# Eight-row transfers for half of three units in the expert stage

## The chip, the cores and the metric

One NeuronCore of a Trainium2 chip runs the whole kernel. The metric is the device time of one execution in microseconds, and the kernel before has a median of 1470.73 us over three runs (1468.03 to 1473.0). One further execution was taken with the hardware profiler; all rows below come from it.

## The reference

Two layers of a hybrid backbone on 256 latent and 256 context tokens of width 1024, all in float32. Each layer has a mixer (attention heads beside a convolution module) and a channel layer: a dense SwiGLU in layer 0, and in layer 1 a top-2-of-8 expert SwiGLU on the latent tokens alone, which is the stage that the change touches:

```python
def swiglu(h, w1, w3, w2):
    return (jax.nn.silu(h @ w1) * (h @ w3)) @ w2

def moe_swiglu(h, w_r, b_r, w1, w3, w2):
    hf = h.reshape(B * L, D)                                   # 256 x 1024
    logits = (hf @ w_r).astype(jnp.float32) + b_r
    top_v, top_i = lax.top_k(logits, TOP_K)                    # 2 of 8
    gates = jax.nn.softmax(top_v, axis=-1)
    combine = jnp.sum(jax.nn.one_hot(top_i, N_EXPERTS) * gates[..., None], axis=-2)
    out = jnp.zeros_like(hf)
    for e in range(N_EXPERTS):
        out = out + combine[:, e:e+1] * swiglu(hf, w1[e], w3[e], w2[e])
    ...
# w1, w3: (8, 1024, 2816), w2: (8, 2816, 1024)
```

The three weight arrays of the eight experts are 8 x 3 x 1024 x 2816 x 4 bytes, 277 MB, and each is read once. After the experts come the residual sum and a last RMSNorm with its store.

## The kernel before, in words

The work of layer 0 and of layer 1's mixer comes first; the expert stage runs from about 795 us to the end. Its weights come through a ring in the on-chip memory that holds 18 pieces, called units (`UNITS_HELD`, `RING_AT`). An expert is cut into three groups of columns (`WIDTH` 768, 1024, 1024), so that there are 24 groups g. A group has eight units of first weights (`H_UNIT[g, p, m]`: w3 and w1 for four pairs of 128-row blocks of the input, 128 partitions x 2 x 768 or 1024 numbers) and three or four units of w2 (`Y_UNIT[g, u]`: 256 rows of w2, 128 partitions x 2 x 1024 numbers, 1 MB). The order, the same for the loads and for TensorE, is the first units of group g, then the w2 units of group g-1. That makes 280 units in a round of the stage (`UNITS`). A second and a third round stand in the program for the case that an expert has more tokens than its slots; they are skipped at run time for these inputs, as the 280 issues in the trace show.

SyncE (SP) issues every unit in this order. `load(v, dst, src)` (lines 596 to 603) first waits until the unit that held the same place, v-18, has been used (`unit_done`), and then issues one transfer of 128 partitions. From the second expert on, the address depends on a register (`expert[e]`), so a few register instructions stand before some transfers. One partition takes two runs of 4096 bytes. A completed transfer adds 16 to the semaphore of the unit's place (`unit_in`).

TensorE waits for that semaphore in `landed_unit(v)` (line 1121), called by `pair` (line 1237, matmuls of L1249) and by `second_unit` (line 1187, matmuls of L1207 and L1215). It adds one to `unit_done` per unit when it is through with it. After the last unit come the scatter (L1174), a sum on VectorE (L2257), the norm (L1786, L1790, L2362) and the store (L641).

Of the kernel before, what the change touches and what calls it, by code (L numbers as in the profile page):

```python
# [11 lines left out]
P = 128  # L12
# [48 lines left out]
UNITS_HELD = len(RING_AT)  # L61
# [25 lines left out]
def unit_numbers():  # L87

    h, y, n = {}, {}, 0
    for g in range(NG + 1):  # L90
        if g < NG:
            for p in range(KT // 2):
                for m in range(2):
                    h[g, p, m] = n
                    n += 1
        if g:
            for u in range(ROW_UNITS[(g - 1) % CH]):
                y[g - 1, u] = n
                n += 1
    return h, y, n  # L100


H_UNIT, Y_UNIT, UNITS = unit_numbers()


def slots(i):
# [28 lines left out]
def backbone(nc, t, out):  # L135
    with ExitStack() as ctx:
# [3 lines left out]
        def sem(name):  # L140
            return ctx.enter_context(nc.semaphore(name))
# [160 lines left out]
        unit_in = [filled[s] if s < SLOTS and third == 0 else sem(f"unit_in_{s}_{third}") for s, third in RING_AT]  # L302
# [103 lines left out]
        unit_base = [level[s] if s < SLOTS and third == 0 else 0 for s, third in RING_AT]  # L406
# [174 lines left out]
        def _(sp):  # L581
# [14 lines left out]
            def load(v, dst, src):  # L596
                if v >= UNITS_HELD:
                    sp.wait_ge(unit_done, v - UNITS_HELD + 1)
                elif v < 8:
                    sp.wait_ge(mx_mm, 2 * IN_TILES)  # L600
                else:
                    sp.wait_ge(L[1]["wo_mm"], 4 if v < 14 else KT)
                sp.dma_start(dst, src).then_inc(unit_in[v % UNITS_HELD], 16)  # L603

            def expert_weights(r):
                expert = {}
# [42 lines left out]
        def _(pe):  # L649
# [88 lines left out]
            for l in range(2):  # L738
# [292 lines left out]
                if l == 0:  # L1031

                    pe.wait_ge(lo_ready, piece_count(1))
                    for k in range(KT):
                        pe.wait_ge(lo_ready, h_count(k))
                        for half in range(2):
                            b = bank[2 * half][:, :]
# [6 lines left out]
                    for n in range(1, NF):  # L1044
# [4 lines left out]
                        for half in range(2):  # L1049
                            h = 2 * n + half  # L1050
                            b = bank[2 * half + n % 2][:, :]
# [67 lines left out]
            mm(bank[4][:, 0:NE], const("ones"), mask[1], start=False, stop=True).then_inc(pos_mm, 1)  # L1119

            def landed_unit(v):
                pe.wait_ge(unit_in[v % UNITS_HELD], unit_base[v % UNITS_HELD] + 16 * (v // UNITS_HELD + 1))

            def gather(r, turn, i_, ps):

# [57 lines left out]
            def second_unit(r, g, u):  # L1183
# [5 lines left out]
                if u == 0:  # L1189
# [3 lines left out]
                    if j == 0 and NE * r + e:  # L1193
                        pe.wait_ge(yt_ready, before(e, r, 1, 2))
                landed_unit(v)
                first, last = j == 0 and u == 0, j == CH - 1 and u == ROW_UNITS[j] - 1

# [1231 lines left out]
```

## Time and profile before

| what | value |
|---|---|
| median of three runs | 1470.73 us (1468.03 to 1473.0) |
| profiled execution, its own time | 1468.3 us |
| its span, first to last instruction | 1466.3 us |
| mean granted TensorE clock | 0.983 |
| TensorE matmuls busy | 1398.3 us, 95% of the span |
| VectorE, ScalarE busy | 541.0 us, 402.8 us |
| units issued by L603 | 280: 216 of 1024 KB, 64 of 768 KB |
| read from HBM | 388.66 MB |

How to read it: a busy matmul row is a union of overlapping matmuls (a matmul occupies a quarter of the array here, and several run at once), so 95% does not say that the engine does all it could. The DMA share is the mean over the core's 16 DMA engines; packets overlap slightly, so that a fully busy stretch reads 1.02 or 1.03. Dividing a share by 1.03 and multiplying by 16 gives how many of the engines were at work.

### The profile page before, as it was taken

How to read it: one execution, taken by the hardware profiler on the slowest of the kernel's cores; microseconds unless marked ns; L12 is line 12 of the kernel's file. 1: busy time of each engine (PE TensorE's matmuls, PEld its weight loads, DVE VectorE, ACT ScalarE, POOL GpSimd, SP SyncE). 2: the span in 40 equal slices, each digit the busy share in tenths (PEclk: the TensorE clock that was granted, in tenths of full speed). 3: DMA queues.
4: the chain of work that ended last, by engine and by line, in shares of the span. 5: the costliest groups of instructions: out<-in, count | busy, mean ns of one | idle time of the engine just before them, and what ended most of it. 6: DMA issues, size and time to landing. Idle time of an engine off the chain costs nothing.

```text
span 1466.3 us, 26038 instructions
## 1 busy us (share of the span) xinstructions
PE 1398.3 (95%) x11437; PEld 823.4 (56%) x11437; DVE 541.0 (37%) x984; ACT 402.8 (27%) x708; POOL 0.2 (0%) x4
## 2 busy tenths in 40 slices
PE   6999889999999999989888999999999999999896
PEld 3788558888888888878676333333333333333231
DVE  3699884523223323469874102111120201101022
ACT  4423584522222322466482101100110101001011
POOL 0000000000000000000000000000000000000000
PEclk8999999999999999999999999999999999999999
DMA  9989903532331043411408999999999999999995
GB/s 351 385 301 345 345 2 115 173 115 72 101 115 58 29 174 113 144 58 58 173 3 343 400 363 409 405 409 405 408 408 406 408 406 409 405 408 408 406 408 234
DMA packets 144984, 391.47 MB, mean 267 GB/s; under 512 B 7104, under 2 KB 38368, under 8 KB 144864
## 3 DMA queue, kind: packets, MB, share of 16 engines
q1 hardware_dynamic: 144032, 388.85, 69.7%
q8 instruction: 93, 1.52, 0.4%
q10 hardware_dynamic: 832, 0.88, 0.2%
q14 instruction: 27, 0.22, 0.0%
HBM read 388.66 MB, written 1.05 MB: 266 GB/s over the span
## 4 chain that ended last, share of the span: by engine, by line
PE 83%; DVE 6%; DMA 6%; SPq 3%; ACT 1%; issue 1%; DVEq 0%; ACTq 0%
PE bank L1249 24%; PE bank L1207 9%; PE bank L1056 5%; PE bank L1055 5%; PE bank L1057 5%; PE bank L760 4%; PE bank L762 4%; PE bank L761 4%; DMA weight_ring<-in_w_ada 3%; DMA weight_ring<-in_exp_w 3%; PE bank L1064 3%; PE bank L1065 3%; PE bank L1066 3%; PE bank L1215 3%; PE bank L709 2%; SPq L603 2%
## 5 line engine op out<-in xcount | busy, mean ns | idle before, releaser
L1249 PE MATMUL bank<-weight_ring,gathered 128*32 128x512 f32 (+1 forms) x3840 | 393.4, 561 | 7.5 <-issue 4.5
L1249 PEld LDWEIGHTS bank<-weight_ring,gathered 128*32 128x32 f32 x3840 | 123.0, 110 | 251.5 <-issue 251.0
L1207 PE MATMUL bank<-weight_ring,scratch 128*32 128x512 f32 x1344 | 157.2, 593 | 0.6 <-DMA weight_ring<-in_exp_w 0.6
L2301 DVE TENSOR_TENSOR scratch<-scratch,bank 64x512 f32<-64x512 f32 (+1 forms) x60 | 38.3, 639 | 260.1 <-ACT scratch L1727 258.1
L1057 PE MATMUL bank<-slot_halves,slot_halves 128*128 128x512 f32 x336 | 130.7, 389 | 0.0
L1056 PE MATMUL bank<-hT_halves,slot_halves 128*128 128x512 f32 x336 | 130.7, 389 | 0.0
L1055 PE MATMUL bank<-slot_halves 128*128 128x512 f32 x320 | 124.6, 389 | 0.0
L1956 DVE SCALAR_TENSOR_TENSOR weight_ring<-scratch,conv_weights,weight_ring 128x512 f32<-128x512 f32 (+1 forms) x207 | 121.1, 637 | 2.2 <-ACT weight_ring L1518 0.3
L761 PE MATMUL bank<-hT_halves,slot_halves 128*128 128x512 f32 (+1 forms) x336 | 114.9, 342 | 0.0
L760 PE MATMUL bank<-slot_halves,slot_halves 128*128 128x512 f32 (+1 forms) x268 | 98.5, 368 | 2.9 <-DVE hT_halves L1838 2.9
L1207 PEld LDWEIGHTS bank<-weight_ring,scratch 128*32 128x32 f32 x1344 | 42.5, 110 | 99.3 <-issue 97.1
L1727 ACT ACTIVATE scratch<-bank 64x512 f32<-64x512 f32 (+1 forms) x60 | 33.4, 557 | 230.0 <-PE bank L1249 229.1
L1842 DVE TENSOR_TENSOR slot_halves<-weight_ring,slot_halves 128x1024 fp32r<-128x1024 f32 x44 | 53.8, 1226 | 107.3 <-ACT slot_halves L1474 107.3
L762 PE MATMUL bank<-slot_halves,slot_halves 128*128 128x512 f32 (+1 forms) x256 | 90.5, 354 | 0.0
L1732 ACT ACTIVATE scratch<-bank 128x512 f32<-128x512 f32 (+1 forms) x23 | 12.9, 560 | 230.1 <-PE bank L1226 230.1
L1057 PEld LDWEIGHTS bank<-slot_halves,slot_halves 128*128 128x128 f32 x336 | 63.1, 188 | 13.1
L1056 PEld LDWEIGHTS bank<-hT_halves,slot_halves 128*128 128x128 f32 x336 | 63.1, 188 | 13.0
L1064 PE MATMUL bank<-slot_halves,slot_halves 128*128 128x512 f32 x176 | 68.6, 390 | 0.3 <-DVE tail_halves L1848 0.3
L761 PEld LDWEIGHTS bank<-hT_halves,slot_halves 128*128 128x128 f32 x336 | 65.0, 193 | 6.8
L1474 ACT ACTIVATE slot_halves<-weight_ring 128x1024 fp32r<-128x1024 f32 x44 | 46.3, 1056 | 79.3 <-PE bank L1057 77.9
L1055 PEld LDWEIGHTS bank<-slot_halves 128*128 128x128 f32 x320 | 60.1, 188 | 12.5
L2257 DVE SCALAR_TENSOR_TENSOR scratch<-bank,softmax_stats,scratch 128x512 f32<-128x512 f32 x32 | 22.5, 746 | 106.3 <-PE bank L1180 57.1
(298 smaller groups left out, 1675.8 us busy)
## 6 DMA issues: line engine op xcount, KB each, us to landing
weight_ring<-in_exp_w SPq DMA_DIRECT2D x216, 1024.0 KB, 16.9
weight_ring<-in_w_ada SPq DMA_DIRECT2D x24, 2048.0 KB, 14.2
weight_ring<-in_exp_w SPq DMA_DIRECT2D x64, 768.0 KB, 14.8
weight_ring<-in_ffn_w SPq DMA_DIRECT2D x33, 1024.0 KB, 5.5
weight_ring<-in_w_out SPq DMA_DIRECT2D x4, 2048.0 KB, 11.5
weight_ring<-in_w_in SPq DMA_DIRECT2D x6, 1024.0 KB, 7.9
weight_ring<-in_w_in SPq DMA_DIRECT2D x2, 3072.0 KB, 17.4
weight_ring<-in_w_in SPq DMA_DIRECT2D x4, 512.0 KB, 14.4
```

The source lines that it names most:

```text
L760: mm(ps, hi, x[l][k][:, 0:T], start=(k == 0), stop=False)
L761: mm(ps, hi, x_lo[k][:, 0:T], start=False, stop=False)
L762: return mm(ps, lo, x[l][k][:, 0:T], start=False, stop=(k == KT - 1))
L1055: mm(b, hi, h_hi[k], start=(k == 0), stop=False)
L1056: mm(b, hi, h_lo[k], start=False, stop=False)
L1057: i = mm(b, lo, h_hi[k], start=False, stop=(k == KT - 1))
L1064: mm(b, hi, a_hi[n % 2], start=(n == 0), stop=False)
L1207: i = mm(bank[6][quarter, :], at01[:, c0:c0 + BLOCK], w2[:, i_, half * 512:(half + 1) * 512], start=(first and i_ == 0), stop=(last and i_ ...
L1249: i = mm(ps[BLOCK * job:BLOCK * (job + 1), 0:cw], gathered_block(e, k, b), w[:, kk, a * cw:(a + 1) * cw], start=(k == 0), stop=(k == KT - 1))
L1474: f(piece_head(h), piece(h), ACT.Copy).then_inc(hi_ready, 1)
L1842: tt(piece(h, True), piece(h), piece_head(h).bitcast(F32), ALU.subtract).then_inc(lo_ready, 1)
L1956: i = stt(out=dst, in0=src, scalar=wk, in1=dst, op0=ALU.mult, op1=ALU.add)
```

## The change

For three of the 280 units, `Y_UNIT[5, 0]`, `Y_UNIT[12, 0]` and `Y_UNIT[19, 0]` (the unit numbers 74, 156 and 237 in the order of the loads), the one transfer of 128 partitions becomes nine: partitions 0 to 63 in eight transfers of eight partitions each (64 KB each), and partitions 64 to 127 in one (512 KB). The bytes and their places are the same. Each of the nine adds 16 to the same semaphore, and TensorE's wait counts all transfers that have gone into that place so far. The numbers of the three units are the same in every round (`v % UNITS`).

```diff
+ROWS_AT_ONCE = 8
+BY_FEW_ROWS = [Y_UNIT[g, 0] for g in (5, 12, 19)]
+
+def transfers_of(v):
+    few = P // 2 if v % UNITS in BY_FEW_ROWS else 0
+    return [(a, a + ROWS_AT_ONCE) for a in range(0, few, ROWS_AT_ONCE)] + [(few, P)]
+
+def transfers_into_place(v):
+    return sum(len(transfers_of(w)) for w in range(v % UNITS_HELD, v + 1, UNITS_HELD))
...
-                sp.dma_start(dst, src).then_inc(unit_in[v % UNITS_HELD], 16)
+                for a, b in transfers_of(v):
+                    sp.dma_start(dst[a:b], src[a:b]).then_inc(unit_in[v % UNITS_HELD], 16)
...
-                pe.wait_ge(unit_in[v % UNITS_HELD], unit_base[v % UNITS_HELD] + 16 * (v // UNITS_HELD + 1))
+                pe.wait_ge(unit_in[v % UNITS_HELD], unit_base[v % UNITS_HELD] + 16 * transfers_into_place(v))
```

On SP, before the change, this stands around the first of the three units (the sixth group's first pieces of 768 columns, then w2 pieces of 1024 columns; `ISA` is a register instruction):

```order
74 L603 DMA weight_ring<-in_exp_w 128x2x768 x2
75 L603 ISA
76 L603 DMA weight_ring<-in_exp_w 128x2x1024
77 L603 ISA
78 L603 DMA weight_ring<-in_exp_w 128x2x1024
79 L603 ISA
```

And with the change, at the same place of the same engine:

```order
74 L617 DMA weight_ring<-in_exp_w 128x2x768 x2
75 L617 ISA
76 L617 DMA weight_ring<-in_exp_w 8x2x1024
77 L617 ISA
78 L617 DMA weight_ring<-in_exp_w 8x2x1024
79 L617 ISA
...
90 L617 DMA weight_ring<-in_exp_w 8x2x1024
91 L617 ISA
92 L617 DMA weight_ring<-in_exp_w 64x2x1024
93 L617 ISA
94 L617 DMA weight_ring<-in_exp_w 128x2x1024
```

Row 76 has become eight transfers of eight partitions and one of 64, each with a register instruction ahead of it; what follows is the same as before, eight issues later. The other two places look alike. No other engine's order changes.

## Rows read from the trace of the kernel before

**Rows 1.** The page, part 2: busy tenths in 40 equal slices of the span.
```profile
PE   6999889999999999989888999999999999999896
DMA  9989903532331043411408999999999999999995
```

**Rows 2.** Windows; columns: stretch, length, busy of each engine, granted clock, DMA share, GB/s.
```profile
860.00:960.00 100.00, 100.00 (x1019) 38.51 (x1015) 17.29 (x32) 12.41 (x24) 0.00 (x0) 1.00 1.03 406
1160.00:1260.00 100.00, 100.00 (x919) 31.64 (x915) 17.04 (x29) 9.71 (x17) 0.00 (x0) 1.00 1.03 407
1360.00:1440.00 80.00, 74.98 (x665) 24.16 (x661) 11.55 (x22) 7.72 (x14) 0.00 (x0) 0.96 1.03 408
```

**Rows 3.** The chain that ended last; columns: start us, us, what.
```profile
1433.57 19.34 DMA weight_ring<-in_exp_w
1452.91 0.04 issue
1452.95 1.97 PE bank L1207 x16
...
1460.91 1.41 DVE scratch L2362 x2
...
1463.19 0.66 DVEq L136
```

**Rows 4.** Waits, 1300 to 1431 us; columns: total us, times, longest.
```profile
PE bank L1249 <- DMA weight_ring<-in_exp_w: 2.4, 1, 2.4
```

**Rows 5.** Waits, 1431 to 1455 us.
```profile
PEld bank L1207 <- DMA weight_ring<-in_exp_w: 7.8, 6, 2.7
PE bank L1207 <- DMA weight_ring<-in_exp_w: 4.1, 5, 1.8
```

**Rows 6.** Windows of 1 us at the end of the loads.
```profile
1440.00:1441.00 1.00, 1.00 (x12) 0.13 (x4) 0.00 (x0) 0.00 (x0) 0.00 (x0) 1.00 1.02 389
1442.00:1443.00 1.00, 1.00 (x12) 0.26 (x8) 0.00 (x0) 0.00 (x0) 0.00 (x0) 1.00 0.70 287
1444.00:1445.00 1.00, 0.70 (x8) 0.34 (x12) 0.00 (x0) 0.57 (x1) 0.00 (x0) 1.00 0.60 242
1447.00:1448.00 1.00, 1.00 (x12) 0.26 (x8) 0.00 (x0) 0.00 (x0) 0.00 (x0) 1.00 0.56 229
1448.00:1449.00 1.00, 0.67 (x8) 0.00 (x0) 0.00 (x0) 0.00 (x0) 0.00 (x0) 1.00 0.53 217
1450.00:1451.00 1.00, 0.53 (x8) 0.24 (x12) 0.00 (x0) 0.00 (x0) 0.00 (x0) 1.00 0.48 197
1452.00:1453.00 1.00, 0.44 (x8) 0.05 (x7) 0.00 (x0) 0.00 (x0) 0.00 (x0) 1.00 0.08 33
```

**Rows 7.** DMA queues, 858 to 1443 us: packets, MB, share of 16 engines.
```profile
q1 hardware_dynamic: 64803, 237.27, 102.1%
q8 instruction: 45, 0.74, 0.5%
q14 instruction: 10, 0.08, 0.0%
```

**Rows 8.** DMA queues, 1444 to 1453 us.
```profile
q1 hardware_dynamic: 371, 1.42, 38.8%
q10 hardware_dynamic: 144, 0.52, 14.9%
q8 instruction: 1, 0.02, 1.0%
q14 instruction: 2, 0.02, 0.6%
```

**Rows 9.** DMA queues, 11 to 18.5 us: the two 124-row loads of L1355 on q10.
```profile
q1 hardware_dynamic: 1295, 2.62, 100.2%
q10 hardware_dynamic: 254, 0.13, 6.1%
```

**Rows 10.** Line L1347, its eight-row loads: ns min/median/max, first and last start.
```profile
L1347 ACTq DMA_DIRECT2D scratch<-in_dw_b x1: 360/360/360, 4.6 to 4.6; - x1
L1347 ACTq DMA_DIRECT2D scratch<-in_conv_ln_g x1: 342/342/342, 4.9 to 4.9; - x1
```

**Rows 11.** Line L603, 930 to 945 us (unit 74 is issued here).
```profile
L603 SPq DMA_DIRECT2D weight_ring<-in_exp_w x6: 372/372/417, 930.5 to 941.6; - x6
DMA to landing us min/median/max: 8.9/10.4/11.4
```

**Rows 12.** Line L603, 1325 to 1345 us (unit 237 is issued here).
```profile
L603 SPq DMA_DIRECT2D weight_ring<-in_exp_w x9: 413/2227/5221, 1322.0 to 1342.4; - x9
DMA to landing us min/median/max: 17.5/18.4/20.9
```

**Rows 13.** Line L603, whole stage.
```profile
DMA to landing us min/median/max: 4.4/16.0/22.0
```

## The prediction

> **What bounds the kernel now.** I read the 40 slices first. From slice 22 on both TensorE and the DMA engines are at nine tenths or more, so the expert stage is where either could be the bound [rows 1]. The windows decide it further: in 860 to 1440 us the DMA share stands at 1.03 in every stretch, 406 to 408 GB/s, which is as full as the 16 engines read [rows 2]. TensorE reads 100 of 100 us too, but that is a union of overlapping matmuls, so I went on to the chain that ended last and the waits. The chain runs from a unit's transfer, issued at 1433.57 and landed 19.34 us later, through the last sixteen w2 matmuls at 1452.95 to the norm and store [rows 3]. TensorE waits for a unit only 2.4 us between 1300 and 1431 [rows 4], and 7.8 + 4.1 us (weight loads and matmuls, the two overlap) between 1431 and 1455 [rows 5]. So the loads have been the longer stream all along, TensorE lives on its stock until 1431, and the end is set by the last landing near 1452.9 plus a fixed tail of 1466.3 - 1452.95 = 13.4 us.
>
> The fine windows of the last loads are the row that matters. All 16 engines work until 1441; then the share falls to 0.70, 0.60, and from 1447 to 1451 it stands at 0.56 to 0.48 [rows 6]. Divided by 1.03 that is 10.9, 9.3, 8.7, 8.2 and 7.5 engines. About half of the engines are through by 1443 and the other half works on until 1452: the load ends uneven, a light half and a heavy half. The 128-partition transfers give each engine the same bytes, so something else fills the heavy half. The candidate is in the queues: 45 instruction packets of 16 KB on q8 pass between 858 and 1443, 0.5% of 16 engines x 585 us = 47 engine-us; if all of them go to the same eight engines that is 5.9 us each, of the same order as the 9 to 10 us seen [rows 7].
>
> **The change, part by part.**
>
> *Bytes moved between engines.* This is the term that decides. A transfer of few rows need not use all 16 engines. Between 11 and 18.5 us two 124-row loads run beside full-rate weight loads; q10 and q1 packets stand 254 to 1295, one to 5.1 [rows 9]. Were the two queues alternating on all 16 engines they would be near one to one; alternating on four engines gives a q1 packet on each of 16 for one of q10 on 4, one to four. So the 124 rows lie on about four engines. No row shows a transfer of eight rows by itself, so its place is bounded: on all 16 engines (nothing moves) or on a set of eight, one row each. I take eight. Then the eight small transfers put partitions 0 to 63, 512 KB, on eight engines (64 KB each), and the 64-partition transfer gives 32 KB to each of the 16. Before, every engine had 64 KB of a unit. The set of eight gets 32 KB more and the others 32 KB less. At 237.27 MB in 585 us on 16 engines [rows 7] one engine moves 25.3 KB per us, so 32.8 thousand bytes are 1.29 us, and three units are 3.9 us: plus for the set, minus for the rest.
>
> The Trainium skill has this rule (DMA: Bandwidth & Descriptors, section on why a DMA increments its semaphore by 16 and not by 1): a transfer issued from SP or ACT runs on the largest number of engines up to 16 that divides its slowest dimension, and on the lowest-numbered ones. For 124 rows that gives four, and the trace agrees [rows 9]; for eight rows it gives engines 0 to 7, which no row here shows. It says nothing of which engines fetch instructions, so it leaves the sign of the change open.
>
> *Which half is the heavy one.* The rows give no engine's number. If the eight small transfers avoid the heavy half altogether, the heavy half ends 3.9 us sooner; if they lie on it, or on a part of it, the worst engines end 3.9 us later. I choose the first and give it 0.6; this is judgement, not a reading.
>
> *Sum for that case.* Heavy half: 1452.9 - 3.9 = 1449.0. Light half: most of it is through by 1443, and would end near 1447. But not all: the share of 9.3 engines at 1444 and 8.7 at 1447 to 1448 says that one light engine works on to about 1447.5 [rows 6]. That one ends at 1447.5 + 3.9 = 1451.4 and is now the last. So the last landing moves from 1452.9 to 1451.4, a gain of 1.5 us, not of 3.9. There is a check from above: in 1444 to 1453 all queues together take 55.3% of 16 engines x 9 us, 79.6 engine-us [rows 8]; spread evenly over 16 that is 5.0 us, an end at 1449.0, so no shift whatever can give more than 3.9 us here. TensorE can follow: it stands idle for more than that in its waits after 1431 [rows 5].
>
> *Issues on SP.* 24 more issues. An eight-row load took 0.34 to 0.36 us on ACT's queue [rows 10], a unit 0.37 us on SP where the queue had room [rows 11]. With the register instruction I take 0.55 us each, eight of them 4.4 us per unit. They delay the issue of the next units by that much at most. At unit 74 a unit lands 8.9 to 11.4 us after its issue, at unit 237 17.5 to 20.9 [rows 11, 12]; a landing takes 4.4 us where nothing is queued [rows 13]. So the engines have 4.5 to 13 us of queued work in front of them, and the delay is covered: cost nothing, and at worst, with the cover gone at unit 74 alone, the 4.4 us less 4.5, still nothing. At 237 SP itself is held by a full queue (2.2 us per issue) and has no time to lose.
>
> *Engine time of small transfers.* The same 256 packets of 4096 bytes; new are completion writes on eight engines. Bounds: 0 below, and above the 0.12 us in which an engine of the 124-row load turned over a small packet beside a large one (7.5 us for 62 packets [rows 9]), 8 x 3 x 0.12 = 2.9 us on the set of eight. I take nothing, because units followed each other at full rate with their completion writes [rows 2]. The upper end would take the 1.5 us away and more: the light engine at 1451.4 would end at 1454.3, 1.4 us later than before.
>
> *Waits.* TensorE's wait counts nine increments of 16 where it counted one; for unit 74 it comes many microseconds after the landing, as the stock of TensorE at that time shows by the absence of waits until 1431 but one [rows 4].
>
> The sum is against the profiled execution's own 1468.3 us: 1466.8. That execution lies 2.4 us under the median of the runs, so for the median 1470.73 - 1.5 = 1469.2 us.
>
> **The rivals.**
>
> *The small transfers lie on the heavy half, or on some of it.* The place is the end of the loads, the price 3.9 us on the engines that end last: 1452.9 + 3.9 = 1456.8, a time of 1474.6, slower by 0.27%. It decides as soon as one heavy engine is in the set. TensorE cannot absorb it, since it waits for every unit after 1431 [rows 5]. For it: nothing in the rows tells the halves apart, and of the ways to pick eight of sixteen most overlap. Against it: the heavy set is a clean half, eight engines, as the steady 8.2 to 8.7 shows, and two clean halves either coincide or exclude each other.
>
> *The small transfers use all 16 engines.* Nothing moves between engines: 0, 1470.7 us. Against it stands the one to five of [rows 9].
>
> *Small transfers cost a latency each.* If each of the 24 stopped its engines for the part of an uncovered landing that is no data (4.4 us less 1.9 us for 768 KB at 407 GB/s, 2.5 us [rows 2, 13]), the engines would lose 24 x 2.5 = 60 us, and the loads are the bound: about 1530 us. Against it: units queued behind each other land at full rate without such gaps, and the 124-row loads ran beside a share of 100.2% [rows 9].
>
> The Trainium skill's table of rules for kernel authors (DMA: Bandwidth & Descriptors) says to coalesce many small transfers, because under 64 KB one pays mostly overhead. The eight-row transfers are exactly 64 KB. The page gives about 2 us of fixed cost; taken 24 times in series that would be 48 us by an estimate from the page. The full-rate rows speak for overlap and against it.
>
> **How the numbers follow.** A favourable half 0.62 (1469.2), unfavourable or mixed 0.24 (1474.6), all 16 engines 0.08 (1470.7), overhead of some kind 0.06 (from 1472 upwards). What a measurement here tells from no change is about 0.3%, 4.4 us. The first case stays within it unless the medians scatter (they ranged over 5 us before): faster 0.12 in all. The second sits just under the bound, so about two in five of it count as slower, with most of the last case: slower 0.16. Within 0.3%: 0.72. The range must hold the first case with up to its 3.9 us bound and the second with its scatter: 1466.0 to 1475.2. The first case's own range is 1466.5 to 1471.
>
> **What would show it right or wrong.** In the changed profile the chain should still end with a unit's transfer and the same 13.4 us behind it. Right: the share in the last loads falls later and more steeply, with few microseconds at half, and the last landing is near 1451.4. Wrong by the second case: the time at a share near 0.5 grows from about 9 to about 17 us, and the end moves by +3.9. Wrong by the third: the same steps at the same times. Wrong by the last: the share dips under 1.0 at 936, 1130 or 1330 us. If SP's extra issues mattered, a wait of TensorE for a unit would appear soon after those times.

## The result, and the profile after

The changed kernel takes 1493.86 us (median of 4 runs, 1491.44 to 1495.47) against 1470.61 us of the kernel before on the same chip (4 runs, 1468.03 to 1473.0): a ratio of 1.0154, 95% interval 1.0139 to 1.017. It is slower by 23.3 us, where 1469.2 was forecast. The profiled execution took 1495.21 us with a span of 1493.1, against 1468.3 and 1466.3 before.

The slices of the page (the same two rows as in [rows 1], with the GB/s row instead of TensorE's) hold the whole story, if they are read together (busy tenths and GB/s in 40 equal slices of the span):

```profile
DMA  9979903533231142510428999999999999999995
GB/s 351 385 282 346 333 1 113 170 113 99 71 113 57 43 183 87 187 39 28 170 109 341 370 398 408 347 408 406 409 406 373 369 404 409 406 408 327 404 409 208
```

From slice 23 on the DMA row stands at 9, but for the last slice, as it did before, so by that row nothing has changed. The GB/s row does not: 347 in one slice, 373 and 369 in two, 327 in one, where the neighbours have 404 to 409. These are the stretches behind the three changed units. The windows of [rows 2] for the kernel after:

```profile
860.00:960.00 100.00, 100.00 (x1011) 38.00 (x1007) 17.29 (x32) 11.79 (x23) 0.00 (x0) 1.00 1.02 385
1160.00:1260.00 100.00, 97.91 (x895) 31.11 (x891) 17.04 (x29) 9.11 (x16) 0.00 (x0) 1.00 1.03 398
1360.00:1440.00 80.00, 74.56 (x667) 24.18 (x667) 12.66 (x24) 7.33 (x13) 0.00 (x0) 0.96 1.02 380
```

Share 1.02 or 1.03 again, but 385, 398 and 380 GB/s for 406, 407 and 408. The engines have as much to do and move less. Closer, in steps of 5 us behind the first changed unit (same columns: stretch, length, busy of TensorE, its weight load, VectorE, ScalarE, GpSimd, granted clock, DMA share, GB/s):

```profile
935.00:940.00 5.00, 5.00 (x42) 2.14 (x42) 0.00 (x0) 1.09 (x2) 0.00 (x0) 1.00 1.03 401
940.00:945.00 5.00, 5.00 (x41) 2.14 (x41) 0.00 (x0) 0.49 (x1) 0.00 (x0) 1.00 1.00 371
945.00:950.00 5.00, 5.00 (x44) 2.17 (x40) 0.00 (x0) 0.49 (x1) 0.00 (x0) 1.00 1.02 216
950.00:955.00 5.00, 5.00 (x47) 2.36 (x47) 1.37 (x2) 1.67 (x3) 0.00 (x0) 1.00 1.01 191
955.00:960.00 5.00, 5.00 (x56) 1.67 (x52) 0.00 (x0) 0.00 (x0) 0.00 (x0) 1.00 1.03 407
```

For some 10 us the engines are full (1.01, 1.02) at half the rate (216, 191 GB/s), and then the rate is whole at once. So a packet takes about twice as long in that stretch; neither a gap nor a starved queue would leave the share at 1.02. The trace's packet records say the same: the 116 packets of 4096 bytes that start between 950 and 953 us take 373 ns at least and 414 ns in the median, where those of the kernel before have a median of 162 ns between 945 and 955 us. So no engine was at its usual pace there. Taken over the three places:

```profile
910.00:970.00 60.00, 60.00 (x539) 22.49 (x539) 5.68 (x9) 6.55 (x12) 0.00 (x0) 1.00 1.02 370
1100.00:1180.00 80.00, 80.00 (x732) 26.43 (x728) 9.24 (x16) 8.44 (x16) 0.00 (x0) 1.00 1.03 372
1310.00:1410.00 100.00, 91.32 (x804) 28.42 (x800) 10.79 (x22) 6.59 (x12) 0.00 (x0) 0.93 1.02 377
```

The same stretches of the kernel before:

```profile
910.00:970.00 60.00, 60.00 (x552) 22.37 (x548) 5.57 (x9) 6.01 (x11) 0.00 (x0) 1.00 1.03 407
1100.00:1180.00 80.00, 80.00 (x744) 26.06 (x740) 9.24 (x16) 7.36 (x14) 0.00 (x0) 1.00 1.03 408
1310.00:1410.00 100.00, 95.50 (x867) 30.23 (x863) 14.19 (x25) 7.93 (x14) 0.00 (x0) 0.97 1.03 407
```

A loss is the length times (1 - rate / 407): 60 x 37/407 = 5.5 us, 80 x 35/407 = 6.9 us, 100 x 30/407 = 7.4 us, together 19.8 us. From here on such a stretch of slow packets is called a dip.

The spans differ by 26.8 us, and the rest is outside the changed units. One part is the start of the expert stage:

```profile
760.00:820.00 60.00, 55.44 (x644) 41.71 (x648) 26.45 (x84) 24.57 (x45) 0.00 (x0) 0.97 0.70 271
```

Before the same stretch moved more:

```profile
760.00:820.00 60.00, 55.51 (x652) 39.26 (x654) 24.04 (x77) 21.34 (x40) 0.00 (x0) 0.97 0.77 298
```

That is 60 x 27/407 = 4.0 us by which the stage starts later. It is no work of the change, for a version that loses nothing in the stage shows it as well (two transfers by run, below):

```profile
760.00:820.00 60.00, 55.46 (x648) 41.66 (x651) 26.22 (x83) 24.38 (x45) 0.00 (x0) 0.97 0.70 270
```

Its profiled execution had 1473.93 us with no other loss; the profiled execution of before was 2.3 us under the median of its four. So executions scatter by some 4 us there, and the 23.3 us between medians hold 19.8 us of dips and 3.5 us more. The last part is the end. The chain, which answers to [rows 3]:

```profile
1460.37 19.34 DMA weight_ring<-in_exp_w
...
1479.76 1.97 PE bank L1221 x16
```

It is built as before: the last unit lands 19.34 us after its issue, as it did there, TensorE's last sixteen matmuls follow, and behind 1479.76 come 13.3 us (13.4 before). What differs is the stream of landings ahead of it. Its last 15 us:

```profile
1465.00:1470.00 5.00, 4.42 (x44) 1.25 (x36) 0.00 (x0) 0.60 (x1) 0.00 (x0) 1.00 0.92 365
1470.00:1475.00 5.00, 3.86 (x40) 0.92 (x32) 0.00 (x0) 1.49 (x2) 0.00 (x0) 1.00 0.48 179
1475.00:1480.00 5.00, 2.62 (x28) 0.57 (x24) 0.00 (x0) 0.00 (x0) 0.00 (x0) 1.00 0.12 47
```

Against before:

```profile
1440.00:1445.00 5.00, 3.77 (x36) 0.89 (x32) 0.00 (x0) 0.57 (x1) 0.00 (x0) 1.00 0.78 313
1445.00:1450.00 5.00, 3.15 (x28) 0.57 (x20) 0.00 (x0) 0.92 (x2) 0.00 (x0) 1.00 0.68 270
1450.00:1455.00 5.00, 3.85 (x32) 0.83 (x32) 0.06 (x1) 0.00 (x0) 0.00 (x0) 1.00 0.20 77
```

Up to the last landing the three stretches after the change are 14.7 us long and hold 7.4 us of work for all 16 engines (5 x (0.92 + 0.48 + 0.12) / 1.03), and before they are 12.9 us long and hold 8.1 us. The idle time of the engines at the end is thus 7.3 us for 4.8, which is 2.5 us more. In steps of 1 us the fall has another shape than before:

```profile
1467.00:1468.00 1.00, 0.96 (x12) 0.05 (x4) 0.00 (x0) 0.00 (x0) 0.00 (x0) 1.00 1.03 397
1470.00:1471.00 1.00, 0.46 (x8) 0.00 (x0) 0.00 (x0) 0.00 (x0) 0.00 (x0) 1.00 0.36 147
1476.00:1477.00 1.00, 0.67 (x8) 0.29 (x12) 0.00 (x0) 0.00 (x0) 0.00 (x0) 1.00 0.13 53
```

The share is full up to 1468 and at 0.36 two microseconds later, where before it stood at 0.56 to 0.48 for 4 us [rows 6]. So the fall is later and steeper, and behind it comes a tail: from 1475 to 1479 us the share is 0.08 to 0.19, which is one to three engines (0.19 x 16 / 1.03) that work on alone. The pieces: 4.0 + 19.8 + 2.5 = 26.3 of the 26.8 us between the spans, and 19.8 + 2.5 of the 23.3 us between the medians.

TensorE now waits for units from 1120 us on (waits of 1120 to 1300; before, the first ended behind 1300 [rows 4]; L1263 and L1221 are the L1249 and L1207 of the kernel before):

```profile
PE bank L1263 <- DMA weight_ring<-in_exp_w: 9.1, 7, 2.1
PEld bank L1221 <- DMA weight_ring<-in_exp_w: 3.5, 3, 1.6
PE bank L1221 <- DMA weight_ring<-in_exp_w: 1.2, 2, 0.7
```

Up to 1120 there is no such wait: the first dip was paid out of TensorE's stock of landed units, the second was not. As the loads are the longer stream, the stock only decides where the wait is seen, not how long the kernel takes.

### The profile page after: what moved, and what is told of

It is laid out like the page before. It is cut to its first block, busy times and chain, and to the rows that moved or that the text cites. A ratio compares the mean times of both kernels' runs of the same rounds, so it can differ in the third digit from the quotient of the medians.

```text
span 1493.1 us, 26110 instructions
## 1 busy us (share of the span) xinstructions
PE 1407.1 (94%) x11437; PEld 827.8 (55%) x11437; DVE 541.2 (36%) x984; ACT 402.7 (27%) x708; POOL 0.2 (0%) x4
## 4 chain that ended last, share of the span: by engine, by line
PE 75%; DMA 10%; DVE 8%; SPq 5%; ACT 1%; issue 1%; DVEq 0%; ACTq 0%
PE bank L1263 21%; DMA weight_ring<-in_exp_w 8%; PE bank L1221 7%; PE bank L1069 5%; PE bank L1071 5%; PE bank L1070 5%; SPq L617 4%; PE bank L774 3%; PE bank L775 3%; PE bank L776 3%; DVE weight_ring L1970 3%; PE bank L1078 3%; PE bank L1080 3%; PE bank L1079 3%; PE bank L723 2%; DMA weight_ring<-in_w_ada 2%
## 5 line engine op out<-in xcount | busy, mean ns | idle before, releaser
L1263 PE MATMUL bank<-weight_ring,gathered 128*32 128x512 f32 (+1 forms) x3840 | 397.1, 564 | 22.5 <-DMA weight_ring<-in_exp_w 17.9
L1263 PEld LDWEIGHTS bank<-weight_ring,gathered 128*32 128x32 f32 x3840 | 125.0, 111 | 269.3 <-issue 268.8
L1221 PE MATMUL bank<-weight_ring,scratch 128*32 128x512 f32 x1344 | 158.0, 593 | 2.6 <-DMA weight_ring<-in_exp_w 2.6
L1221 PEld LDWEIGHTS bank<-weight_ring,scratch 128*32 128x32 f32 x1344 | 42.3, 110 | 102.4 <-issue 93.7
L1746 ACT ACTIVATE scratch<-bank 128x512 f32<-128x512 f32 (+1 forms) x23 | 12.9, 561 | 241.9 <-PE bank L1240 241.9
L1071 PEld LDWEIGHTS bank<-slot_halves,slot_halves 128*128 128x128 f32 x336 | 63.1, 188 | 13.2
L1070 PEld LDWEIGHTS bank<-hT_halves,slot_halves 128*128 128x128 f32 x336 | 63.1, 188 | 13.2
```

The source lines that it names most:

```text
L1070: mm(b, hi, h_lo[k], start=False, stop=False)
L1071: i = mm(b, lo, h_hi[k], start=False, stop=(k == KT - 1))
L1221: i = mm(bank[6][quarter, :], at01[:, c0:c0 + BLOCK], w2[:, i_, half * 512:(half + 1) * 512], start=(first and i_ == 0), stop=(last and i_ ...
L1263: i = mm(ps[BLOCK * job:BLOCK * (job + 1), 0:cw], gathered_block(e, k, b), w[:, kk, a * cw:(a + 1) * cw], start=(k == 0), stop=(k == KT - 1))
```

## The experiments

All but a2 and a3 keep the kernel's arithmetic; a2 and a3 put rows of w2 into other partitions than the matmuls expect, so that their sum is another one, while the instructions and the bytes are the same. Except where bytes are said to be added or other units are named (b3, c1, c3), they change only how `transfers_of` cuts the same three units (74, 156 and 237). P is 128, and the code is shown shortened. "Loss" is worked out from windows as above, in the one profiled execution of each. a2, a3, b4 and c2 have two executions each, the others four to ten.

**Neighbours or not (a1 to a4).** The eight small transfers take eight neighbouring partitions each, and their sources lie together too. a1 takes every fourth partition for both:

```diff
-    [(a, a + 8) for a in range(0, 64, 8)] + [(64, P)]
+    [slice(a + h, a + h + 29, 4) for h in (0, 32) for a in range(4)] + [slice(64, P)]
```

> The eight transfers of eight partitions take every fourth partition (0, 4, ... 28, then 1, 5, ...; and the same from 32) instead of eight neighbours, and the matching rows of the weights; number, size and the eight engines stay. Theory W or R (eight neighbouring partitions, or eight neighbouring rows, are what slows the packets): the dip of the DMA rate near 944 to 955 us is gone and the loss of 23.3 us with it; what is left is the shift of bytes between engines, -1.5 us by the prediction's first case (1469) or +3.9 us by its rival (1474.5). Theory N (24 small transfers cost by their number or size): still +20 to +25 us (1491 to 1496).

a2 writes neighbours and reads rows four apart, a3 the reverse:

```diff
+    near, far = [slice(a, a + 8) for a in range(0, 64, 8)], [slice(a + h, a + h + 29, 4) ...]
+    list(zip(near, far)) + [(slice(64, P), slice(64, P))]     # a2: to near, of far
+    list(zip(far, near)) + [(slice(64, P), slice(64, P))]     # a3: to far, of near
```

> Eight neighbouring partitions as in the change, but filled from every fourth row of the weights (w2's rows come to other partitions, so the sum of the three units is another one). Theory W (the writes into neighbouring partitions are slow): +20 to +25 us, packets of 300 to 430 ns as in the change. Theory R (the reads of neighbouring rows are slow): no loss, 1467 to 1475. Theory N: +20 to +25.

> Every fourth partition, filled from neighbouring rows (again w2's rows come to other partitions). Theory W: no loss, 1467 to 1475. Theory R: +20 to +25 us. Theory N: +20 to +25.

a4 has no small transfer at all:

```diff
+    [slice(0, 64), slice(64, P)]
```

> The same three units as two transfers of 64 partitions each. No small transfer and nothing moved between engines. Theory W: 64 neighbouring partitions on 16 engines are written by twice as many engines per place of the memory as 128 are, so each half goes at half rate: 2.6 us lost per unit where the two follow each other strictly, +7.7 us for three at most, and some of it is also in the change's own loss. Theory R or N: 0 to +1 us.

| kernel | median, us | before beside it | ratio, 95% interval | GB/s in 910-970, 1100-1180, 1310-1410 | loss, us |
|---|---|---|---|---|---|
| after | 1493.86 | 1470.61 | 1.0154 [1.0139, 1.017] | 370, 372, 377 | 19.8 |
| a1, step of 4 | 1485.84 | 1470.03 | 1.0115 [1.0097, 1.0132] | 375, 382, 391 | 13.5 |
| a2, near partitions | 1495.96 | 1470.03 | 1.0177 [1.0157, 1.0198] | 369, 373, 373 | 20.7 |
| a3, near rows in memory | 1484.04 | 1470.03 | 1.0096 [1.0076, 1.0116] | 376, 383, 391 | 13.2 |
| a4, two halves | 1489.62 | 1470.03 | 1.0131 [1.0114, 1.0148] | 380, 377, 377 | 17.3 |

a2 stands with the changed kernel and a3 with a1: it is where the packets are written that matters, not where they are read. None of the theories had a1's time: it is 15.8 us over before, between no loss and the whole. And a4 says that most of the loss needs no small transfer: two halves cost 19.6 us, where 7.7 us was the most that was expected. In its window at the first unit:

```profile
940.00:945.00 5.00, 5.00 (x44) 2.14 (x45) 0.00 (x0) 0.49 (x1) 0.00 (x0) 1.00 1.04 324
945.00:950.00 5.00, 5.00 (x41) 2.18 (x40) 0.00 (x0) 0.49 (x1) 0.00 (x0) 1.00 1.04 223
950.00:955.00 5.00, 5.00 (x49) 1.59 (x52) 1.37 (x2) 1.67 (x3) 0.00 (x0) 1.00 1.01 360
```

Again a full share and half the rate. a1 has a mark of another kind besides: its strided issues cost SP 0.70 us (median of its 27 issues there), where an issue of eight neighbours costs 0.28, and at the first unit, where little is queued, the engines starve for a moment (share 0.52):

```profile
945.00:950.00 5.00, 5.00 (x41) 2.14 (x41) 0.00 (x0) 0.49 (x1) 0.00 (x0) 1.00 0.52 127
```

Over the whole first place a1's share is 0.98:

```profile
910.00:970.00 60.00, 60.00 (x539) 22.03 (x541) 5.56 (x8) 6.40 (x12) 0.00 (x0) 1.00 0.98 375
```

That is 60 x 0.05/1.03 = 2.9 us of engines without work, so about 10.6 of a1's 13.5 us are slow packets.

**Two transfers of another cut (b1, b2), one unit (b3), quarters (b4).** If a second transfer cost something, b1 and b2 would show it: b1 sends all 128 partitions twice, one 4096-byte run each, b2 the even partitions and then the odd ones.

```diff
+    sp.dma_start(dst[:, q, :], src[:, q, :])    # b1, for q = 0, 1
+    [slice(0, 127, 2), slice(1, 128, 2)]        # b2
+    BY_FEW_ROWS = [Y_UNIT[19, 0]]               # b3, cut as in the change
+    [slice(a, a + 32) for a in range(0, P, 32)] # b4
```

> The three units as two transfers of 512 KB, as in a4_two_halves, but each goes to all 128 partitions: the first run of 4096 bytes of every partition, then the second. Number and size are those of a4, only the set of partitions differs. Theory H (a transfer that goes to one half of the partitions is slow, whatever its size): no loss, 1468 to 1472. Theory N (a second and smaller transfer costs): the +19.6 us of a4 again, 1488 to 1491.

> Two transfers of 64 partitions, the even ones and then the odd ones, so that each reaches over the whole memory. Theory H, if what counts is how much of the memory a transfer reaches in all: no loss. If what counts is what the engines write at the same moment: some loss, up to the +19.6 us of a4_two_halves. Theory N: +19.6.

> The change for Y_UNIT[19, 0] alone (unit 237). If each unit costs by itself: a third of the change's 23.3 us, +6 to +9 (1476 to 1479). If the loss is made by SP's issues running out of cover at unit 74: near 0. If the first units' loss makes the later ones worse: under 6.

> The three units as four transfers of 32 neighbouring partitions. Theory H (32 neighbours reach as many ways into the memory as 64 do): about the loss of a4_two_halves, +17 to +23 us. Theory N: twice that of a4 or more, +35 to +60. If the loss goes by the share of partitions reached: also about twice.

| kernel | median, us | before beside it | ratio, 95% interval | GB/s at the three places | loss, us |
|---|---|---|---|---|---|
| b1, two by run | 1472.77 | 1471.17 | 1.0005 [0.9994, 1.0016] | 406, 407, 407 | 0 |
| b2, even then odd | 1469.75 | 1471.17 | 0.9995 [0.9983, 1.0006] | 407, 408, 407 | 0 |
| b3, unit 237 alone | 1477.84 | 1471.17 | 1.0046 [1.0029, 1.0062] | 406, 407, 372 | 8.6 |
| b4, quarters | 1486.42 | 1471.17 | 1.0105 [1.0085, 1.0125] | 380, 375, 380 | 16.9 |

b2's row is the one to set beside a4's. Both are two transfers of 64 partitions, 512 KB each, of the same packets:

```profile
910.00:970.00 60.00, 60.00 (x552) 22.32 (x548) 5.56 (x8) 5.53 (x10) 0.00 (x0) 1.00 1.03 407
```

No loss with even and odd, 6.5 us per unit with lower and upper half. Quarters cost 15.3 us, somewhat less than halves and than the 17 to 23 us expected; that four transfers cost no more than two speaks against a price per transfer. One changed unit alone costs about a third of three (6.7 of 23.3 us), so the price is paid unit by unit.

**Eight rows spread wide (c1 to c3).** Eight rows at a step of 16 over all partitions, and the even partitions in one transfer. c2 does it at the units of the change, c1 at groups 12, 16 and 19, where more is queued in front of the engines, c3 at six units.

```diff
+    [slice(a, a + 113, 16) for a in range(1, 16, 2)] + [slice(0, 127, 2)]
+    for g in (12, 16, 19)               # c1;  (5, 12, 19) in c2;  (12, 13, 15, 16, 18, 19) in c3
```

> Eight transfers of eight partitions a, a+16, ... a+112 (a odd), and one of the 64 even partitions, so that every transfer reaches over the whole memory; on the units 156, 194 and 237, where a unit lands 17 us or more after its issue. Theory H (only transfers kept to one half of the partitions, or closer, are slow): the 23 us are gone and the shift of bytes between engines is left alone: -1.5 us if the eight engines of an eight-row transfer are the light ones, +3.9 us if they are the heavy ones. If eight partitions at a distance of 16 still reach too few ways: a part of the loss stays, +3 to +8 us.

> As c1_wide_eights_covered, on the units 74, 156 and 237 of the change. At unit 74 a unit lands only 9 to 11 us after its issue, and a transfer with a step took SP 0.7 us in a1_step4_both, 0.9 us from one to the next, 8 x 0.9 = 7 us. Theory S (SP's issues run out of cover there): 2 to 5 us slower than c1, with a dip of the DMA share under 1.0 near 945 us. Otherwise the same as c1.

> As c1_wide_eights_covered, on six units. Shift of 7.7 us instead of 3.9. If the eight engines are the light ones, they become the late ones: last landing 1447.4 + 7.7 = 1455, +2 us against before, and +3.7 against c1. If they are the heavy ones: +7.7. If each eight-row transfer costs by itself: twice the loss of c1.

| kernel | median, us | before beside it | ratio, 95% interval | GB/s in 1100-1430 |
|---|---|---|---|---|
| before | | | | 407 |
| c1, three units | 1488.11 | 1470.55 | 1.0106 [1.0088, 1.0124] | 390 |
| c2, the change's units | 1483.35 | 1470.55 | 1.0087 [1.0066, 1.0107] | 396 |
| c3, six units | 1502.65 | 1470.55 | 1.0212 [1.0194, 1.0229] | 371 |

Spreading did not help, and six units cost 32.1 us, 5.4 us each. c2's first unit lies outside the column: it has 382 GB/s in 910 to 970, 3.7 us more. c2 was expected 2 to 5 us over c1 and came out 4.8 us under it. The share did dip at its first unit (0.80 in 945 to 950), but the place cost no more than c1's middle one (393 GB/s in 1180 to 1310, 4.5 us). In c3 the share is 1.01 over the 330 us, so up to 6.4 us of its loss (330 x 0.02/1.03) are engines without work. I had hoped to balance the two halves of the engines with that; what these kernels lose is far over the 3.9 us that balance could bring. Left open was whether eight rows cost by themselves or by the partitions that their eight engines hit: with the step of 16 the engines of a small transfer also meet each other and the other half's partitions.

**Extra transfers beside untouched units (d, e).** These leave all 280 units whole and add transfers beside five of them (groups 14, 16, 18, 20, 22), into a part of `scr` that nothing reads, so bytes are added and nothing is re-cut. TensorE's wait for the unit counts the added transfers too:

```diff
+    for rows in [None] + (EXTRA if v % UNITS in FIVE_UNITS else []):
+        to, of = (dst, src) if rows is None else (scr[rows, D:2 * D], src[rows, 0, :])
+        sp.dma_start(to, of).then_inc(unit_in[v % UNITS_HELD], 16)
+EXTRA = [slice(a + h, a + h + 29, 4) for h in (0, 32) for a in range(4)]     # d1
+EXTRA = [slice(a + h, a + h + 29, 4) for h in (64, 96) for a in range(4)]    # d2
+EXTRA = [slice(a, a + 8) for a in range(0, 64, 8)]                           # d3
+EXTRA = [slice(0, 64)]                                                       # d4
+EXTRA = [slice(0, 127, 2)]                                                   # e1
+EXTRA = [slice(0, P)]                                                        # e2
+EXTRA = [slice(a, a + 57, 8) for a in range(8)]                              # e3
```

> All 280 units are loaded as before, each by one transfer of 128 partitions. Beside five of them (Y_UNIT[g, 0] for g = 14, 16, 18, 20, 22) eight transfers of eight rows more run, with the first 4096 bytes of the unit in partitions 0 to 63, each at a step of 4 partitions (a, a + 4, ..., a + 28), into a part of scr that nothing reads. So nothing is loaded less: 64 packets of 4096 bytes are added to a unit, 8 on each of eight engines, 8 x 0.159 us = 1.27 us, for five units 6.4 us of those eight engines. Theory A (a packet costs more where an engine writes partitions that are another engine's in the ordinary transfer, or where several write neighbours): here each of the lower eight engines writes one row of its own set in each transfer, no dip of the rate beside the five units, the eight engines end at 1447.5 + 6.4 = 1453.9 against 1452.9 before, so 1470.5 + 1.0 = 1471.5 us. Theory B (eight rows at a step cost by themselves, whatever partitions they write): five dips of about half those of the step-4 kernel, 2.2 us each, 1470.5 + 1 + 11 = 1482 us.

> The same five times eight extra transfers of eight rows at a step of 4, but with the rows of partitions 64 to 127, into those partitions. If the eight engines are the same as in the run on partitions 0 to 63, they now write the other eight engines' partitions. Theory A: dips beside the five units, at most those of the first kernel's per byte (about 3 us for a unit's extra half), 1475 to 1485 us, and clearly above the run on partitions 0 to 63. Theory B: the same time as that run.

> The same five times eight extra transfers in partitions 0 to 63, but each of eight neighbouring partitions, so that eight engines write eight neighbours at once. Theory A (neighbours slow each other): the change with neighbours lost 8 us more than that with a step of 4, for 3 units of 128 such packets of 4096 bytes; here five units of 64 packets each: 8 x 320 / 384 = 6.7 us over the run with a step of 4, so about 1478 us. Theory B (any eight rows cost alike): the same time as with a step of 4.

> Five extra transfers of 64 partitions (0 to 63, first 4096 bytes of the unit), one beside each of the same five units, on all 16 engines: 4 packets on each engine, 4 x 0.159 = 0.64 us, for five 3.2 us of all engines, heavy ones too, so without any slower packet 1470.5 + 3.2 = 1473.7 us. Theory A (a half's packets put two engines on each set of partitions): six halves of 512 KB lost 19.6 us, 3.3 us each; these are 256 KB, 1.6 us each, so 8 us more, 1482 us. Theory B (only transfers of eight rows lose): 1473.7 us.

> As in the run with one extra transfer of 64 partitions beside each of five units (256 KB, 4 packets on each of 16 engines, same source size), but the 64 rows are the even partitions 0, 2, ..., 126 instead of 0 to 63. If what costs is how many engines write into the same set of partitions, these spread as the ordinary transfer does and only the packets' own 5 x 4 x 0.159 = 3.2 us of all engines remain: 1471.2 + 3.2 = 1474.4 us, no dip of the rate. If a transfer of 64 rows costs by itself, 1486 us as with partitions 0 to 63.

> The extra transfer beside each of the five units covers all 128 partitions (first 4096 bytes of each, 512 KB): twice the bytes of the other extras, in the ordinary shape. Own engine time 5 x 8 x 0.159 = 6.4 us on all engines: 1471.2 + 6.4 = 1477.6 us, no dip. So if where the packets are written is what costs, twice the bytes are 8 us cheaper than the half on partitions 0 to 63 (1486); if added bytes or added transfers cost, it is dearer than that, above 1490.

> The eight extra transfers of eight rows in partitions 0 to 63, now at a step of 8 partitions (a, a + 8, ..., a + 56). The run with a step of 4 gave 1476.5, with neighbours 1487.6. By the assignment of sets of 4 + 4 partitions (p and p + 32 in one set), a step of 4 puts one engine on a set, a step of 8 two, neighbours four. If the price goes with how many engines meet on a set it lies between the two, near 1482; if only neighbouring partitions hurt, 1476.5; if any departure from each engine's own set costs in full, 1487.6.

| kernel | bytes added | median, us | before beside it | ratio, 95% interval | GB/s in 1160-1430, loss |
|---|---|---|---|---|---|
| d1, eights, step 4, in 0-63 | 5 x 256 KB | 1476.47 | 1471.34 | 1.0037 [1.0024, 1.0051] | 404, 2.0 us |
| d2, eights, step 4, in 64-127 | 5 x 256 KB | 1487.66 | 1471.34 | 1.011 [1.0084, 1.0136] | 391, 10.6 us |
| d3, eights of neighbours | 5 x 256 KB | 1487.64 | 1471.34 | 1.011 [1.0082, 1.0137] | 395, 8.0 us |
| e3, eights, step 8, in 0-63 | 5 x 256 KB | 1486.27 | 1472.39 | 1.0095 [1.0075, 1.0115] | 395, 8.0 us |
| d4, partitions 0-63 | 5 x 256 KB | 1485.96 | 1471.34 | 1.0104 [1.0079, 1.0128] | 393, 9.3 us |
| e1, even partitions | 5 x 256 KB | 1475.67 | 1472.39 | 1.0015 [1.0004, 1.0026] | 407, 0 |
| e2, all partitions | 5 x 512 KB | 1478.1 | 1472.39 | 1.0032 [1.0018, 1.0045] | 407, 0 |

Four of the five extras lie in the last column's stretch. Two pairs decide. d4 and e1 add the same number of bytes, rows and transfers, both on a destination that nothing reads. d4's window, with partitions 0 to 63:

```profile
1160.00:1430.00 270.00, 259.04 (x2358) 82.44 (x2350) 38.92 (x69) 22.94 (x41) 0.00 (x0) 0.97 1.03 393
```

And e1's, with the even partitions:

```profile
1160.00:1430.00 270.00, 262.14 (x2426) 83.89 (x2420) 38.93 (x69) 23.51 (x42) 0.00 (x0) 0.99 1.03 407
```

Same share, 393 against 407 GB/s; 14.6 us against 3.3, of which 3.2 is the extra data. e2 adds twice as much in the ordinary shape and costs 5.7 us, forecast 6.4. The other pair is d1 and d2, the same eight-row transfers in the lower and in the upper half:

```profile
1160.00:1430.00 270.00, 261.55 (x2398) 83.48 (x2394) 38.93 (x69) 22.92 (x41) 0.00 (x0) 0.98 1.02 404
```

d2's window reads:

```profile
1160.00:1430.00 270.00, 257.47 (x2350) 81.97 (x2345) 38.91 (x69) 22.94 (x41) 0.00 (x0) 0.97 1.02 391
```

11.2 us lie between them, so eight rows do not cost that by themselves. Which partitions they are is what costs. Steps of 4, 8 and 1 in partitions 0 to 63 give +5.1, +13.9 and +16.3 us: a step of 8 costs nearly the whole price, and by the reading below that is where two engines of a small transfer first meet. I had expected the middle one halfway (1482), and that is not so. Neighbours (d3) were expected near 1478 and came out 10 us over it, the half (d4) 4 us over its 1482, and d2 3 us over its 1475 to 1485.

The reading that fits all: in an ordinary transfer each engine has a set of eight partitions of its own, and while two engines write into one set, packets are slow, and not only those two engines': 191 of 407 GB/s is less than eight engines at their full rate alone would move, and in 950 to 953 us of the changed kernel no packet of 4096 bytes took under 373 ns. The Trainium skill names the sets. "DMA: Bandwidth & Descriptors", section "The descriptor swizzle", gives the engine of a partition p in a 128-partition transfer as 8 x (p >> 6) + ((p >> 2) & 7), so engine 0 has 0 to 3 and 32 to 35, and the lower eight engines have 0 to 63.

How the rows of a smaller transfer are dealt out is my assumption, as no row names an engine: the eight rows of a small one in their order to the eight lower engines, the 64 rows of a half or of the even partitions in the pattern of the whole. Then a step of 4 in 0 to 63 (d1) puts each of eight engines on its own set, a step of 8 (e3) two on one, neighbours (d3) four on one, a half (d4, a4) 16 engines on eight sets, and d2 puts the lower engines on the upper engines' sets; b1, b2, e1 and e2 leave every engine its own. The runs agree in every case: 0 to 2.0 us of loss where each is on its own set, 8.0 us and more elsewhere. So it is shown that the partitions written decide the price (a4 and b2, d4 and e1, d1 and d2); that engines meeting on a set are the reason is the reading that fits, and not shown by itself.

**Where d1's time goes.** d1 was expected at 1 us over before and came out 5.1 over [3.5, 7.5 by its ratio]. 2.0 us are in its window, where the share is 1.02 instead of 1.03. The added bytes are 3.2 us of all engines' time (1.31 MB at 407 GB/s), and the forecast counted on the light half's spare time at the end to take most of that. Its end is steeper indeed, as more packets on the light half would make it:

```profile
1450.00:1455.00 5.00, 4.24 (x36) 0.98 (x34) 0.00 (x0) 0.60 (x1) 0.00 (x0) 1.00 1.02 406
1455.00:1460.00 5.00, 3.85 (x32) 0.92 (x32) 0.00 (x0) 1.49 (x2) 0.00 (x0) 1.00 0.65 254
1460.00:1465.00 5.00, 2.70 (x24) 0.70 (x28) 0.00 (x0) 0.00 (x0) 0.00 (x0) 1.00 0.09 35
```

Yet the idle time at the end did not shrink: in steps of 1 us the share is 0.12 to 0.15 from 1460 to 1463, about two engines that work on alone, and up to the last landing at 1464.2 us the idle time comes to 5.7 us, for 4.8 before. 2.0 + 3.2 + 0.9 = 6.1 us, near the 5.1 measured. Beside e2, where all engines have more:

```profile
1450.00:1455.00 5.00, 4.20 (x40) 1.25 (x36) 0.00 (x0) 0.60 (x1) 0.00 (x0) 1.00 0.91 360
1455.00:1460.00 5.00, 3.85 (x36) 0.92 (x32) 0.00 (x0) 1.49 (x2) 0.00 (x0) 1.00 0.70 281
1460.00:1465.00 5.00, 2.63 (x24) 0.57 (x24) 0.00 (x0) 0.00 (x0) 0.00 (x0) 1.00 0.34 138
```

No kernel here beats the one before: b2, the best, stands at 0.9995 [0.9983, 1.0006].

## Why the prediction was wrong

**The bound** was read rightly. The loads set the end, and a time lost on the engines came out one to one: 19.8 us of dips in a difference of 23.3. The chain has the same end and the same 13.3 us behind it.

**The step that failed** is "Engine time of small transfers". It took the same 256 packets of 4096 bytes to cost the same, "I take nothing", with 2.9 us as its upper end. It measured 19.8 us, packets that take twice as long and more. The step counted packets and completion writes and had no term for the place that a packet is written to. The upper end came from a row in which 124 rows were loaded beside other loads at a share of 100.2% [rows 9], called full rate on that ground. The row's own bytes give (2.62 + 0.13) MB in 7.5 us, 367 GB/s, with packets of 2 KB on average in q1; the step used its share and its packet counts and not its rate. A slow packet of 4096 bytes it could not have shown either way, as 20 to 40 us of the same kernel also have 370 GB/s without a transfer of that kind. The same holds for the reason given, that units follow each other at full rate with their completion writes [rows 2]: all those units are of 128 partitions, by the map above each engine on its own set, so the rows say nothing on any other shape.

The larger part of the loss was not even in the eight transfers that the step was about. The 64-partition transfer beside them, which the prediction only used to count bytes (32 KB per engine), does it as well: a4 with two such halves loses 17.3 us, and a1, where by the reading above the eight small transfers lie on their engines' own sets and only partitions 64 to 127 go as a half, 13.5 us, some 2.9 of them engines without work. The neighbours add the other 6.3 us (19.8 - 13.5; 8 us between the medians), or some 9 us if slow packets alone are set against each other (19.8 - 10.6).

The Trainium skill had a rule that I did not weigh. "SBUF — State Buffer", section "Door 1: The DMA port swizzle (why [64,N] ≈ [32,N])", says that a transfer to partitions 0 to 63 reaches only eight of the 16 ports and measured 196 GB/s where 128 partitions had 328. The trace agrees with the halved rate: 216 and 191 GB/s in 945 to 955. Set to this unit, the rule gives less than was paid. By rows: 1 MB at 407 GB/s is 2.6 us, and at half the rate twice that, so 2.6 us lost for a unit in two halves, 7.7 for three, or 1478; a4 lost 17.3 us. That the dip lasts for 8 to 10 us and so takes in the ordinary transfers behind is shown by the windows; why it does was not tried.

**Bytes moved between engines.** The direction was right, and it had been chosen by judgement (0.6), so that was luck. All kernels with eight-row transfers fall more steeply at the end than all without: in the microsecond that begins some 3 us before the last landing the share is 0.12 to 0.24 in the twelve of them (the change, a1 to a3, b3, c1 to c3, d1 to d3, e3), and 0.47 to 0.52 in the other eight (before, a4, b1, b2, b4, d4, e1, e2). a4 in that place:

```profile
1468.00:1469.00 1.00, 1.00 (x12) 0.13 (x4) 0.00 (x0) 0.00 (x0) 0.00 (x0) 1.00 0.51 209
```

So the eight-row transfers lie on the engines that were through early, as the first case said, and its sign (a later and steeper fall, few microseconds at half) did appear. The gain of 1.5 us that should follow did not: the idle time of the engines at the end grew by 2.5 us, because one to three engines work on alone for 4 us. Which engines those are, and why, no row tells; the step had one light engine as the last, at 1451.4. c1 to c3 were the attempt to isolate the term, and they lose more than it can bring.

**Issues on SP.** Forecast at 0.55 us each and covered, so that they would cost nothing. The issues of 925 to 970 us in the changed kernel (counts; min, median and max in ns):

```profile
L617 SPq DMA_DIRECT2D weight_ring<-in_exp_w x26: 277/373/3853, 927.7 to 968.5; - x26
DMA to landing us min/median/max: 10.3/16.8/21.1
```

A small issue takes 0.28 us (the least of the 26). The share stays at 1.00 to 1.03 throughout the first dip, so the engines never lacked work: covered, as forecast. With the strided ones of a1, at 0.70 us, the cover does run out once (share 0.52 above); the bound of 4.4 against 4.5 us was as thin as it looked.

**Waits.** The nine increments cost nothing: up to 1120 us, behind the first changed unit, TensorE waits for no unit at all.

**The rivals.** "Small transfers cost a latency each" had the right sign and the wrong mechanism. Its 60 us were idle time of engines, and the share shows none; and b1's and b2's six transfers cost nothing. Its chance of 0.06 was too small because it was the only case that let a transfer of another shape cost engine time, and it was worked out as a gap, not as a rate. Of the marks named beforehand, "the share dips under 1.0 at 936, 1130 or 1330 us" looked in the right places at the wrong number. The one that would have told is GB/s at a full share. The overhead of about 2 us that was taken from the Trainium skill's page is fitted there to transfers issued from GpSimd, and these are issued from SP. The rule weighed among the rivals from the Trainium skill ("DMA: Bandwidth & Descriptors", table of rules for kernel authors), that transfers under 64 KB are mostly overhead, is not what the runs show in this queue: d1's 40 transfers of 32 KB cost 5.1 us in all, 3.2 us of it for their bytes.

## What to carry to other kernels

Where loads are the bound, cut a transfer by columns or by even and odd partitions, which was free here (b1, b2); by halves, quarters or neighbouring rows it cost 5 to 9 us for a unit of 1 MB. By the reading above this is because every engine keeps the partitions that it has in the whole transfer. Read GB/s beside the DMA share, always: a full share says that the engines are occupied, not that they move data at their rate. And a cost bounded by rows of one shape of transfer bounds nothing for another shape; if no row has the shape, the upper end must be a slower packet for all that is queued near it, not only a completion write.

## What the runs showed that was not expected

- Five 256 KB transfers to partitions 0 to 63 cost 14.6 us, five to the even partitions 3.3 us, and five of twice the bytes to all partitions 5.7 us.
- The slow stretch outlasts the transfer that sets it off: about 10 us at 191 to 216 GB/s is 2 MB, twice the unit. Why was not tried. In d4 four extras of 256 KB lost 9.3 us, 2.3 us each, while their own 0.64 us at half the rate would be 0.64 us more.
- By the assumed dealing of rows, two engines on a set are nearly as dear as four: +13.9 us (step of 8) and +16.3 us (neighbours), with intervals that overlap.
- Rows at a step in the partitions cost SP more to issue. Transfers of d1, at a step of 4:

```profile
L620 SPq DMA_DIRECT2D scratch<-in_exp_w x40: 644/645/6402, 1193.8 to 1435.6; - x40
```

  And of d3, with neighbours:

```profile
L620 SPq DMA_DIRECT2D scratch<-in_exp_w x40: 277/277/5367, 1193.8 to 1440.6; - x40
```

  The medians are 645 and 277 ns for the same 32 KB.
